# Attention's query blocks in falling instead of rising length

## The reference

```python
for l in range(2):
    proj = x @ w_in[l]
    o_a = dilated_mixture(...)   # A: 6 heads of 64, three causal windows mixed
    o_b = diff_attention(...)    # B: 4 heads, softmax(q1 k1) - lam * softmax(q2 k2), causal
    o_c = causal_attention(...)  # C: 6 heads of 96, causal
    h = layer_norm(ALPHA * x + concat(o_a, o_b, o_c) @ w_o[l])
    x = layer_norm(ALPHA * h + (silu(h @ w_gate) * (h @ w_up)) @ w_down)
```

## Time and profile before

| | |
|---|---|
| median of 3 runs | 2933.22 us (2933.2 to 2933.54) |
| profiled execution, own time | 2934.33 us |
| its span, first to last instruction | 2932.2 us |
| PE busy | 2900.4 us, 99% |
| DVE busy | 1953.8 us, 67% |
| ACT busy | 1285.1 us, 44% |
| POOL busy | 271.5 us, 9% |
| granted clock of PE, mean | 0.999 |

### The profile page before, as it was taken

How to read it: one execution, slowest core, us unless ns; L and a number is a source line. 1 busy time by engine, 2 the same in 40 slices (tenths; PEclk the granted TensorE clock), 3 DMA queues, 4 the chain that set the end, 5 groups by cost and what they waited for, 6 DMA issues and landing times.

```text
span 2932.2 us, 39072 instructions
## 1 busy us (share of the span) xinstructions
PE 2900.4 (99%) x16334; PEld 2474.8 (84%) x16334; DVE 1953.8 (67%) x2860; ACT 1285.1 (44%) x1988; POOL 271.5 (9%) x222
## 2 busy tenths in 40 slices
PE   8999999999999999999999999999999999999998
PEld 6766899977667999979999998888888888889997
DVE  4576777864757677685646556667777793577675
ACT  4554354434635454463324244443343325354444
POOL 0232000030230000110000000100101021000000
PEclk9999999999999999999999999999999999999999
DMA  5114424441124323212121213121212133322232
GB/s 193 45 56 168 158 98 160 155 164 65 44 103 155 105 101 108 95 72 87 58 72 66 72 65 108 58 90 57 94 47 94 49 117 129 121 85 98 101 108 80
DMA packets 45200, 285.81 MB, mean 97 GB/s; under 512 B 5151, under 2 KB 5679, under 8 KB 19552
## 3 DMA queue, kind: packets, MB, share of 16 engines
q1 hardware_dynamic: 40464, 255.08, 24.9%
q0 software_dynamic: 4560, 28.23, 2.6%
HBM read 277.50 MB, written 5.79 MB: 97 GB/s over the span
## 4 chain that ended last, share of the span: by engine, by line
PE 93%; DVE 3%; ACT 2%; DMA 1%; issue 1%; POOL 0%; SPq 0%; DVEq 0%; POOLq 0%; ACTq 0%
PE ps L866 19%; PE ps L868 19%; PE ps L867 19%; PE ps L1121 10%; PE ps L1123 10%; PE ps L1122 10%; PE ps L1039 2%; PE ps L1052 1%; PE ps L1066 1%; PE ps L965 1%; DVE wlo L2050 1%; DMA MW<-wstream 1%; PE ps L892 0%; PE ps L888 0%; ACT whi L1383 0%
## 5 line engine op out<-in xcount | busy, mean ns | idle before, releaser
L2050 DVE TENSOR_TENSOR wlo<-wraw,whi 128x1536 fp32r<-128x1536 f32 (+2 forms) x220 | 421.8, 1917 | 216.0 <-ACT whi L1383 215.9
L1383 ACT ACTIVATE whi<-wraw 128x1536 fp32r<-128x1536 f32 (+2 forms) x220 | 351.4, 1597 | 459.2 <-PE ps L868 396.5
L866 PE MATMUL ps<-A1h,whi 128*128 128x512 f32 x1024 | 412.0, 402 | 8.8 <-DVE A1l L2081 8.7
L868 PE MATMUL ps<-A1h,wlo 128*128 128x512 f32 x1024 | 400.5, 391 | 0.0
L867 PE MATMUL ps<-A1l,whi 128*128 128x512 f32 x1024 | 400.3, 391 | 0.0
L1121 PE MATMUL ps<-A1h,whi 128*128 128x256 f32 (+1 forms) x836 | 245.5, 294 | 2.5 <-ACT ps L1680 1.5
L1123 PE MATMUL ps<-A1h,wlo 128*128 128x256 f32 (+1 forms) x836 | 244.8, 293 | 0.0
L1122 PE MATMUL ps<-A1l,whi 128*128 128x256 f32 (+1 forms) x836 | 244.7, 293 | 0.0
L866 PEld LDWEIGHTS ps<-A1h,whi 128*128 128x128 f32 x1024 | 193.6, 189 | 51.7 <-issue 12.0
L868 PEld LDWEIGHTS ps<-A1h,wlo 128*128 128x128 f32 x1024 | 192.8, 188 | 41.1
L867 PEld LDWEIGHTS ps<-A1l,whi 128*128 128x128 f32 x1024 | 193.3, 189 | 38.9 <-issue 2.2
(11 more groups left out here) (532 smaller groups left out, 7192.5 us busy)
## 6 DMA issues: line engine op xcount, KB each, us to landing
wraw<-wstream SPq DMA_DIRECT2D x159, 1024.0 KB, 4.9
wraw<-wstream SPq DMA_DIRECT2D x42, 768.0 KB, 4.4
wraw<-wstream SPq DMA_DIRECT2D x34, 640.0 KB, 3.8
MW<-wstream SPq DMA_DIRECT2D x20, 1024.0 KB, 7.6
MW<-wstream POOLq DMA_DIRECT2D x14, 1024.0 KB, 5.9
wraw<-wstream SPq DMA_DIRECT2D x4, 960.0 KB, 5.3
TB<-gd POOLq DMA_DIRECT2D x1, 2560.0 KB, 13.3
X<-xT SPq DMA_DIRECT2D x4, 512.0 KB, 7.6
```

Source lines behind the costliest of these rows:

```text
L866: mm(o, l[0], r[0], start=start, stop=False)
L868: return mm(o, l[1], r[0], start=False, stop=stop)
L1383: act(whi[i_ % 2][:, 0:n], wraw[i_ % 2][:, 0:n], ACT.Copy, bias=0.0, scale=1.0).then_inc(ev("hi", i_).by(act_whi), 1)
L2050: tt(wlo[i_ % 2][:, 0:n], wraw[i_ % 2][:, 0:n], raw(whi[i_ % 2][:, 0:n]), SUB).then_inc(ev("lo", i_).by(dve_wlo), 1)
```

## The change

The four query blocks of each pair of heads are taken in the order 3, 2, 1, 0 instead of 0, 1, 2, 3. The last block of a pair is then block 0, so `pv` follows block 0, and the events that stood for "the last item" are named anew. Nothing else changes: the same instructions with the same shapes, the same fillers in the same steps, the same number of banks.

```diff
-    items = [(kd, h, i) for kd in "BAC" for p in range(0, kinds[kd][0], 2) for i in range(4) for h in (p, p + 1)]
+    items = [(kd, h, i) for kd in "BAC" for p in range(0, kinds[kd][0], 2) for i in (3, 2, 1, 0) for h in (p, p + 1)]
...
-        if 0 <= step - 5 < n and items[step - 5][1] % 2 and items[step - 5][2] == 3:
+        if 0 <= step - 5 < n and items[step - 5][1] % 2 and items[step - 5][2] == 0:
...
-                        e.wait_ge(b.full, ev("prob", l, "B", 3, 3))
+                        e.wait_ge(b.full, ev("prob", l, "B", 3, 0))
...
-                e.wait_ge(ev("w landed", i), ev("used", i - 2), ev("prob", key[1], "A", 4, 3) if key[0] == "woAB" and key[2] == 0 else None)
+                e.wait_ge(ev("w landed", i), ev("used", i - 2), ev("prob", key[1], "A", 4, 0) if key[0] == "woAB" and key[2] == 0 else None)
...
-                        e.wait_ge(ev("prob", key[1], "B", 3, 3))
+                        e.wait_ge(ev("prob", key[1], "B", 3, 0))
...
-                    e.wait_ge(ev("min", l, "C", 5, 3, 0))
+                    e.wait_ge(ev("min", l, "C", 5, 0, 0))
```

## The result

The changed kernel takes 2937.89 us (median of 20 runs, 2936.6 to 2938.79) against 2933.47 us before (20 runs, 2932.7 to 2935.05). The ratio is 1.0014, 95% interval [1.0008, 1.002]: slower by 4.4 us. I had forecast 2931.5 us, faster by 1.7, with a range up to 2936.5. So the direction was wrong and the range too narrow.

A forecast was written before the change was run, and what follows sets the result against it. PE was taken as the bound, with only its waits movable. Per layer -1.37 - 0.31 - 0.18 + 0.74 + 0.28 = -0.84 us, -1.7 over two, gave 2931.5 us from 2933.2; range 2929.0 to 2936.5.

The forecast's parts named there:

- What bounds the kernel, and what can move: Whole kernel: PE is busy 99% of the span; the change leaves its work the same, so only its waits can move.
- The bounds: Attention of both layers: PE is idle for 4.69 us, a first bound on any gain, 0.16%.
- The two waits at step 0, 1.37 us: Transposes behind a new pair's first scores: PE's stalls of 0.69 and 0.68 us go, 1.37 us a layer removed.
- the wait beside A's first scores: Transposes of B's last pair: PE has longer scores ahead of them, so 0.31 us a layer is removed.
- the one at the last `pv`: Last `pv` of C: the copy it waits for is now of one tile, so 0.18 us a layer is removed.
- kind B, for which I had put nothing: B's own items: they stand among 3 fillers each, so nothing was counted there.
- The lag of 0.74 us at `pv` of A0: `pv` of A0: PE comes 0.21 us sooner, the last copy 0.53 us later; 0.74 us a layer added, paid once.
- Steps 4 to 7: Second half of a pair's eight steps: DVE's lag peaks at +0.86 us in step 4; steps 5 to 7 give it back.
- the stall at C's scores: Scores of step 6 of C's second pair: a bank wait of 0.28 us grows, 0.28 us a layer added.
- The rival "POOL blocks DVE": DVE's `probs` against POOL's pieces: a collision costs 1.1 us; two more a layer make 2935.9 us; chance 0.10.
- That which one starts first sets the cost, and not the length of the `probs`: DVE and GpSimd sharing ports: a longer `probs` coming second is no worse than a short one; no size given.

The follow-up runs named there:

- both collisions out of the way: Changed kernel with GpSimd's conversions of `uq` and of the second `w_o` panel each waiting until a named `probs` of DVE is done: 2932.64 us.
- the hold of `uq`: Changed kernel with GpSimd's conversion of `uq` waiting until DVE's probabilities of A, head 2, block 3 are done: 1.5 us above the kernel before.
- for `w_o` there is: Kernel before, all kinds rising, with GpSimd's second `w_o` panel waiting for the probabilities of C, head 1, block 2: 2933.28 us.
- another kernel: Kernel before, rising order, with DVE's probabilities of A, head 2, block 0 waiting for the end of `uq`'s conversion: +7.0 us.

## Why the prediction was wrong

- *What bounds the kernel, and what can move.* Right. The same work, only waits moved, and all of the change lies in attention.
- *The bounds.* The bound on a gain, 4.7 us, held. For a loss I had none but the rivals, and took it too close.
- *The two waits at step 0, 1.37 us.* Right: neither is in the profile after. Gone too are the wait beside A's first scores (119.76 before; 0.24 us from start to start after) and the one at the last `pv`. But the first of these two, 0.31 us in my sum, wasn't a gain: with B alone falling it is gone as well, and attention is 0.1 us longer. So about 0.4 us came in elsewhere in kind B, for which I had put nothing.
- *The lag of 0.74 us at `pv` of A0.* The mechanism is right. Once the collision is out of the way, the waits of `pv` are 0.32 and 0.40 us, against 0.19 and nothing before: 0.53 us, paid in part at both.
- *Steps 4 to 7.* Here the working stopped too early. By my own running sums DVE is at +0.46 us at the end of step 6 and PE at -0.11, so the transposes of step 7 lose 0.57 us of margin, and in rising order those of the tight pair had almost none. I had looked at step 0 and at `pv` alone. The trace has it:
```profile
173.78 0.49 PE L1039 MATMUL ps<-KA,QA 64*128 64x128 f32 x4
174.20 0.55 PE L1052 MATMUL ps<-mats,PP 128*128 128x128 f32 x3
175.46 0.52 PE L1052 MATMUL ps<-mats,PP 128*128 128x128 f32 x3 [0.71 <-DVE PP L2152]
```
  With this wait (+0.71), two waits of 0.2 for a bank that ACT still reads (+0.4), `pv` (+0.53), and the stall at C's scores, which went (-0.28) where I had it grow, the account of the order alone is 0.71 + 0.4 + 0.53 - 1.37 - 0.31 - 0.18 - 0.28 = -0.50 us a layer. Measured, with both collisions out of the way: -0.2. Predicted: -0.84. With B at its measured +0.1 in place of the -0.31 the account makes -0.1.
- *The rival "POOL blocks DVE".* This is the step that failed: in my sum collisions stood at nothing. The rival had the mechanism, the price of 1.1 us for a collision, and even the number of those that PE would wait for, two a layer; measured, they cost 1.2 and 1.0 us a layer, 4.4 in all. But I gave it 0.10, on the ground that a collision must first fall ahead of something that PE needs, and never looked where GpSimd's instructions start. The start of `uq`'s conversion stands 0.05 us behind a `probs` that has `pv` right behind it, in the one place where I had just worked out a shift of tenths of a microsecond. With order and collisions each at its measured worth over both layers, -0.5 and +4.4, the time would have come out at 2937.
- *That which one starts first sets the cost, and not the length of the `probs`.* Right: a 512-key `probs` lost 1.2 us, a 384-key one 1.0 and a 128-key one 1.05; the same rule, turned around, gives the repair.
- *The clock* was in no case of mine. It adds 1.7 us when it falls.

**A and C together.** A alone is worth about +0.15 us a layer without its collision, B +0.1 and C -1.4, which makes about -1.15; together they are worth -0.23. Of the 0.9 us between, 0.7 can be seen. Between A2 and C one wait of some 0.7 us stands if A falls (in its last step, with C falling or rising) or if A and C both rise (at C's start), and none only if A rises and C falls. So C's order removes it only with A rising.

**Not settled:** in what share of executions the clock falls; the other 0.2 us between the parts and the whole; where B lost what it gained; and whether the hold of `uq` does anything in rising order, for which there is no run (for `w_o` there is).

## What to carry to other kernels

Where two engines take turns at a port, look in the trace for the pair that starts within a tenth of a microsecond of each other and has something critical queued behind it; a change of order that shifts either by less than an instruction decides who waits, and 0.12 us of shift cost 1.2 us here. Give such a pair an order by a wait, so that the long background piece starts behind the critical one: two waits won back the whole loss. The wait moves the collision to a later instruction (1.24 and 1.30 us here), so look at what is queued behind that one too. And when lengths are reordered in a pipeline, follow the running difference through all steps of a period, not only through those that stall today.

## What the runs showed of the hardware

- A `probs` of DVE (128x512, 0.46 us free) takes up to 1.67 us when it starts 0.07 us behind a GpSimd conversion of 1.46 us, and a shorter one 1.32 us when it starts 0.02 us behind a subtraction. Started 0.05 us ahead of the conversion, one of 128 keys took its free 0.27 us.
- The granted clock fell to its lower level for some 3.4 us behind a wait of PE of 1.53 us in one execution and of 2.85 us in another kernel, each time in layer 1 and not behind the same wait in layer 0; in a second execution of the first kernel, and with A alone falling, the same wait of 1.53 us stood in both layers and it didn't fall at all. The Trainium skill, "TensorE: Matmul & The Clock Gate", part 1, says that the lower level is the default and that activity releases it. These profiles agree so far: PE had been busy for 0.47 of the 2 us before the fall, and the clock came back while `pv` ran, 0.5 us ahead of its end. They don't show what decides between a fall and none. One fall costs 1.7 us: `pv` took 4.07 us instead of 2.37.
